# First attention of a hybrid encoder: weights turned by VectorE in 32x32 blocks and moved by DMA in place of TensorE transposes

## What is computed

```python
z = einsum('bhqd,bkhd->bhqk', qi, k) * scale
mask = kpos[None, :] < qpos[:, None]
log_1m = where(mask, log_sigmoid(-z), 0.0)
suffix = cumsum(log_1m, axis=3, reverse=True) - log_1m
w = where(mask, exp(log_sigmoid(z) + suffix), 0.0)
out = einsum('bhqk,bkhd->bqhd', w, v)
```

## Time and profile before

| | |
|---|---|
| median of three runs | 1105.87 us (1105.68 to 1105.93) |
| the profiled execution's own time | 1106.12 us |
| its span, first to last instruction | 1104.3 us |
| TensorE busy | 1096.4 us, 99% of the span |
| VectorE busy | 646.1 us, 59% |
| ScalarE busy | 472.8 us, 43% |
| GpSimd busy | 9.6 us, 1% |
| data moved by DMA | 105.11 MB, 95 GB/s on average |
| granted TensorE clock | 0.999 of full speed |

### The profile page before, as it was taken

The page is one execution under the profiler, slowest core; times in us unless marked ns, Lnnn a source line. Parts: engine busy times, 40 slices in busy tenths (PEclk is TensorE's granted clock), DMA queues, the critical chain, the costliest instruction groups (busy, mean ns, idle before and its releaser), DMA issues.

```text
span 1104.3 us, 14616 instructions
## 1 busy us (share of the span) xinstructions
PE 1096.4 (99%) x5336; PEld 900.5 (82%) x5336; DVE 646.1 (59%) x812; ACT 472.8 (43%) x705; POOL 9.6 (1%) x28
## 2 busy tenths in 40 slices
PE   9999999999999999999999999999999999999998
PEld 7788777888888888888888887888888888888886
DVE  6454456656777777763335567656777777762232
ACT  5547437444434444432223456634434444431132
POOL 2000000000000000000000000000000000000000
PEclk9999999999999999999999999999999999999999
DMA  5333131322222222233335221222233222323322
GB/s 199 134 115 96 39 96 39 112 97 92 99 97 95 95 95 95 78 84 100 91 99 159 75 77 58 77 86 90 99 101 100 95 95 95 95 77 119 102 85 77
DMA packets 33017, 105.11 MB, mean 95 GB/s; under 512 B 3905, under 2 KB 4562, under 8 KB 32978
## 3 DMA queue, kind: packets, MB, share of 16 engines
q1 hardware_dynamic: 32258, 103.58, 28.9%
q10 hardware_dynamic: 720, 0.99, 0.3%
HBM read 100.36 MB, written 2.10 MB: 93 GB/s over the span
## 4 chain that ended last, share of the span: by engine, by line
PE 96%; ACT 1%; DVE 1%; DMA 1%; issue 1%; SPq 1%; DVEq 0%; ACTq 0%
PE ps L1318 30%; PE ps L1320 30%; PE ps L1319 29%; PE ps L1517 1%; PE ps L1538 1%; PE ps L1635 1%; PE ps L1660 1%; DMA w_raw<-w_mix 1%; PE ps L1530 1%; PE ps L1645 1%; DVE ssq L954 1%; SPq L507 0%; PE ps L1589 0%; PE ps L1456 0%; PE ps L1577 0%
## 5 line engine op out<-in xcount | busy, mean ns | idle before, releaser
L1318 PE MATMUL ps<-h_hi,w_hi 128*128 128x512 f32 x888 | 349.7, 394 | 0.3 <-DVE h_lo L959 0.3
L1320 PE MATMUL ps<-h_hi,w_lo 128*128 128x512 f32 x888 | 345.9, 390 | 0.0
L1319 PE MATMUL ps<-h_lo,w_hi 128*128 128x512 f32 x888 | 345.7, 389 | 0.0
L655 ACT ACTIVATE w_hi<-w_raw 128x1024 fp32r<-128x1024 f32 (+2 forms) x136 | 135.9, 999 | 420.7 <-PE ps L1320 420.7
L941 DVE TENSOR_TENSOR w_lo<-w_raw,w_hi 128x1024 fp32r<-128x1024 f32 (+2 forms) x136 | 156.0, 1147 | 168.2 <-ACT w_hi L655 167.8
L1318 PEld LDWEIGHTS ps<-h_hi,w_hi 128*128 128x128 f32 x888 | 166.7, 188 | 36.5 <-issue 1.5
L1320 PEld LDWEIGHTS ps<-h_hi,w_lo 128*128 128x128 f32 x888 | 166.7, 188 | 35.1
L1319 PEld LDWEIGHTS ps<-h_lo,w_hi 128*128 128x128 f32 x888 | 166.8, 188 | 34.1 <-issue 0.5
L1109 DVE TENSOR_TENSOR us<-ps,rinv 128x512 f32<-128x512 f32 x88 | 60.7, 692 | 83.4 <-PE ps L1320 83.4
L662 ACT ACTIVATE w_hi<-w_raw 128x1024 fp32r<-128x1024 f32 x47 | 49.3, 1056 | 72.4 <-PE ps L1320 72.2
L947 DVE TENSOR_TENSOR w_lo<-w_raw,w_hi 128x1024 fp32r<-128x1024 f32 x47 | 57.2, 1221 | 35.1 <-ACT w_hi L662 35.0
(11 more groups left out here) (219 smaller groups left out, 1329.8 us busy)
## 6 DMA issues: line engine op xcount, KB each, us to landing
w_raw<-w_up SPq DMA_DIRECT2D x88, 512.0 KB, 3.3
w_raw<-w_mix SPq DMA_DIRECT2D x51, 512.0 KB, 3.4
w_raw<-w_down SPq DMA_DIRECT2D x22, 512.0 KB, 3.3
w_raw<-w_down SPq DMA_DIRECT2D x16, 384.0 KB, 3.1
w_raw<-w_down SPq DMA_DIRECT2D x16, 320.0 KB, 2.9
x<-xT SPq DMA_DIRECT2D x8, 256.0 KB, 6.5
out<-x SPq DMA_DIRECT2D x6, 256.0 KB, 2.0
w_raw<-w_mix SPq DMA_DIRECT2D x4, 256.0 KB, 5.4
```

What stands on the lines that cost most here:

```text
L655: s.activation(w_hi[r % SPL][:, 0:cols], w_raw[r][:, 0:cols], ACT.Copy).then_inc(w_hi_ready, 1)
L1318: mm(dst, w[0], m[0], start=first, stop=False, skip_group_check=shared)
L1319: mm(dst, w[0], m[1], start=False, stop=False, skip_group_check=shared)
L1320: return mm(dst, w[1], m[0], start=False, stop=last, skip_group_check=shared)
```

## The change

VectorE turns each head's weights in 32x32 blocks (`v.transpose`) into a new tile, `sbT`, which lies where `oc_lo` lies later. A 32x32 block is then right in itself but stands in the wrong row group, so SyncE issues 16 transfers a head (`move`), one for each pair of row groups: 32 partitions by ten blocks by 32 words, from `sbT` to `sbW`. The TensorE step "turn" and ScalarE's copy are gone. VectorE's next transpose waits for the transfers of the head before. "pv" reads the blocks in the order that they now have, with five matmuls a head.

The mask is no longer added to the scores. GpSimd sets the blocks on the diagonal of `sbG` to zero on and above it, with two selects a head, after ScalarE's second sigmoid and before VectorE's product; `sbR` holds ones on and above the diagonal, so that the scan gives one there.

Loads of the first mixer's units from the sixth on are issued by ScalarE at the step "split" in place of SyncE. SyncE's swaps and moves stand in one order, worked out from the list (`swap_at`). `EVENTS0` is new. At the start the first two units come in three pieces each, one of them issued by ScalarE, x comes first and from a layout with whole blocks, and there are 11 warm-up matmuls. The diff, cut to its core:

```diff
-EVENTS0 = ((0, "split", 2), (16, "sq", 0), (16, "sq", 1), (21, "split", 3), (24, "ssq", 0), (26, "split", 4),
...
+EVENTS0 = ((7, "split", 2), (20, "sq", 0), (25, "split", 3), (26, "sq", 1), (26, "split", 4), (28, "ssq", 0),
+           (31, "split", 5), (32, "rinv", 0), (33, "split", 6), (35, "left", 0), (37, "z", 0), (44, "split", 7),
+           (44, "z", 1), (46, "split", 8), (53, "move", 0), (53, "left", 1), (55, "split", 9), (76, "split", 10),
+           (76, "split", 11), (76, "split", 12), (89, "pv", 0), (89, "move", 1), (89, "z", 2), (89, "gt", 0),
+           (90, "gz", 0), (92, "left", 2), (93, "split", 13), (96, "gz_v", 0), (97, "split", 14), (102, "split", 15),
+           (102, "move", 2), (105, "gs", 0), (106, "z", 3), (106, "left", 3), (109, "gd", 0), (109, "move", 3),
+           (115, "split", 16), (115, "z", 4), (122, "left", 4), (122, "split", 17), (123, "gd_v", 0),
+           (125, "split", 18), (127, "left", 5), (127, "pv", 1), (127, "z", 5), (132, "split", 19), (138, "move", 4),
+           (146, "split", 20), (153, "split", 21), (157, "move", 5), (161, "gkv_v", 0), (162, "gkv", 0),
+           (162, "z", 6), (163, "left", 6), (166, "split", 22), (170, "gkv_v", 1), (171, "split", 23),
+           (172, "go_v", 0), (174, "move", 6), (174, "gkv", 1), (174, "pv", 2), (177, "go", 0), (181, "go", 1),
+           (181, "z", 7), (181, "go_v", 1), (182, "gn", 0), (183, "left", 7), (184, "gn_v", 0), (188, "split", 24),
+           (188, "gn", 1), (189, "split", 25), (196, "silu", 0), (199, "gout", 0), (199, "move", 7),
+           (200, "split", 26), (201, "pv", 3), (201, "gn_v", 1), (202, "silu", 1), (212, "gout", 1))
...
-def swap_before(j):
-
-    steps = [(name, i) for name, i, _ in SEQ0]
-    before = steps[:steps.index(("z", 2 * j - 1))] if j else []
-    running = max([i for name, i in before if name == "unit"], default=0)
-    return max(running, MIX0.index(("kb", j))) + RAW + 1
+def swap_at(j):
+
+    keys = max(n for n, step in enumerate(SEQ0) if step[:2] in [("unit", MIX0.index((w, j))) for w in ("qb", "kb")])
+    before = [n for n, step in enumerate(SEQ0) if step[:2] == ("z", 2 * j - 1)]
+    return max([keys] + before) + 1
...
-ZOFF = (0, 640, 1024, 512)
-ZW = (512, 384, 256, 128)
+OWN_PAIRS = ((128, 384), (768, 256))
+PV_PARTS = ((0, 0, 3, 0), (0, 896, 1, 3), (1, 128, 3, 0), (2, 256, 2, 0), (3, 384, 1, 0))
...
+        before_gla = ExitStack()
+        sbT = sb("sbT", [P, ZN], F32, before_gla)
+        before_gla.close()
...
-        WARM = 14
+        N_CONSTS = 18
+        WARM = 11
...
+        PIECES = (slice(0, 2 * P), slice(2 * P, 4 * P), slice(4 * P, UC))
+        BLOCK_PIECE = {0: 0, 2: 1}
 
         def load_x(engine, c):
 
-            engine.dma_start(x[:, c, :], xT[:, c * T:(c + 1) * T]).then_inc(x_loaded[c], 16)
-
-        def load_half(engine, u, half):
-
-            engine.dma_start(w_raw[u][:, W_HALVES[half]], w_mix0[u][:, W_HALVES[half]]).then_inc(
-                w_loaded[u] if half else half_loaded[u], 16)
-
-
+            engine.dma_start(x[:, c, :], xT[c]).then_inc(x_loaded[c], 16)
+
+        def load_piece(engine, u, n):
+
+            engine.dma_start(w_raw[u][:, PIECES[n]], w_mix0[u][:, PIECES[n]]).then_inc(
+                w_loaded[u] if n == 2 else piece_loaded[u][n], 16)
...
-            load_half(sp, 0, 0)
             load_x(sp, 0)
-            load_half(sp, 1, 0)
-            for c in (1, 2, 3):
+            load_piece(sp, 1, 0)
+            load_x(sp, 1)
+            load_piece(sp, 0, 1)
+            load_piece(sp, 1, 1)
+            for c in (2, 3):
                 load_x(sp, c)
-            load_half(sp, 0, 1)
+            load_piece(sp, 0, 2)
             load_x(sp, 4)
-            load_half(sp, 1, 1)
+            load_piece(sp, 1, 2)
...
+            def move(i):
+
+                sp.wait_ge(sb_turned, i + 1)
+                sp.wait_ge(sb_pv, i // 2)
+                to, turned = (t[:, :].rearrange("p (n q) -> p n q", q=P) for t in (sbWs[i % 2], sbT))
+                for a in range(TT):
+                    for b in range(TT):
+                        sp.dma_start(to[quad(b), :, quad(a)], turned[quad(a), :, quad(b)]).then_inc(sb_moved, 16)
+
+            unit(RAW, 0, w_mix0[RAW])
+            for at, (name, i, _) in enumerate(SEQ0):
                 for j in range(SH // 2):
-                    if u == swap_before(j):
+                    if at == swap_at(j):
                         swap_halves(j)
+                if name == "move":
+                    move(i)
+            for u in range(N0 + SPL + RAW - 1, U_UP0):
...
-                last = QOFF[i] + (i + 1) * P - 1
-                step(g.memset(sbR[:, last:last + 1], 1.0))
+                own = sbR[:, QOFF[i] + i * P:QOFF[i] + (i + 1) * P]
+                step(g.affine_select(out=own, in_=own, compare_op=ALU.is_gt, fill=1.0,
+                                     base=0, pattern=[[-1, P]], channel_multiplier=1))
...
+            inverse_root(0)
+            for i in range(SH):
+                pool.wait_ge(sb_gate, i + 1)
+                for at, stride in OWN_PAIRS:
+                    own = sbG[:, at:at + 2 * stride].rearrange("p (a k) -> p a k", a=2)[:, :, stride - P:stride]
+                    ins = g.affine_select(out=own, in_=own, compare_op=ALU.is_gt, fill=0.0,
+                                          base=0, pattern=[[0, 2], [-1, P]], channel_multiplier=1)
+                    ins.then_inc(sb_masked, 1)
+            for norm in range(1, 2 * LAYERS):
+                inverse_root(norm)
...
+            load_piece(act, 0, 0)
...
+            first_h_hi(0)
+            piece_hi(0, 0)
+            piece_hi(1, 0)
+            first_h_hi(1)
...
+                    u = i + RAW - 1
+                    act.wait_ge(w_lo_ready, u - (RAW - 1))
+                    act.dma_start(w_raw[u % RAW][:, :], w_mix0[u]).then_inc(w_loaded[u % RAW], 16)
                     hi_static(i)
...
-                    act.wait_ge(sb_z, i + 1)
+                    act.wait_ge(sb_z, TT * (i + 1))
+                    act.wait_ge(sb_weight, i)
                     s.activation(sbA[:, 0:ZN], zs[:, 0:ZN], ACT.Sigmoid, scale=-1.0).then_inc(sb_rest, 1)
+                    act.wait_ge(sb_turned, i)
                     s.activation(sbG[:, :], zs[:, 0:ZN], ACT.Sigmoid).then_inc(sb_gate, 1)
-                elif name == "turn":
-                    act.wait_ge(sb_turned, i + 1)
-                    act.wait_ge(sb_pv, i // 2)
-                    s.activation(sbWs[i % 2][:, :], zs[:, 0:ZN], ACT.Copy).then_inc(sb_w, 1)
...
-                    dve.wait_ge(sb_gate, i + 1)
+                    dve.wait_ge(sb_masked, 2 * (i + 1))
                     v.tensor_tensor(sbG[:, :], sbG[:, :], sbA[:, 1:ZN + 1], ALU.mult).then_inc(sb_weight, 1)
+                    dve.wait_ge(sb_weight, i + 1)
+                    dve.wait_ge(sb_moved, MOVED * i)
+                    v.transpose(sbT[:, :], sbG[:, :]).then_inc(sb_turned, 1)
...
+                        dve.wait_ge(sb_moved, MOVED * SH)
...
-                    pe.wait_ge(consts_dve, 1)
-                    pe.wait_ge(sb_w, i)
+                    pe.wait_ge(sb_gate, i)
...
-                           start=b != 0, stop=False, skip_group_check=True)
-                    for b in range(TT):
-                        diag_block = QOFF[b] + b * P
-                        ins = mm(zs[:, diag_block:diag_block + P], ident_bf[:, :], negmask[:, :],
-                                 start=False, stop=True, skip_group_check=True)
-                    ins.then_inc(sb_z, 1)
-                elif name == "turn":
-
-                    pe.wait_ge(sb_weight, i + 1)
-                    for b in range(TT):
-                        for k in range(b + 1):
-                            at, src = ZOFF[k] + (b - k) * P, QOFF[b] + k * P
-                            ins = nc.tensor.transpose(zs[:, at:at + P], sbG[:, src:src + P], ident[:, :])
-                    ins.then_inc(sb_turned, 1)
+                           start=b != 0, stop=True, skip_group_check=True).then_inc(sb_z, 1)
                 elif name == "pv":
-                    pe.wait_ge(sb_w, 2 * i + 2)
+                    pe.wait_ge(sb_moved, MOVED * (2 * i + 2))
                     pe.wait_ge(oc_lo_ready, i)
-                    for b in range(TT):
+                    for b, at, n, to in PV_PARTS:
                         for hh, w in enumerate(sbWs):
                             h = 2 * i + hh
-                            ins = mm(ps[SD * hh:SD * hh + SD, B_O, b * P:T], vb[:, b, h * SD:(h + 1) * SD],
-                                     w[:, ZOFF[b]:ZOFF[b] + ZW[b]], start=b == 0, stop=b == TT - 1)
+                            cells = w[:, at:at + (n - 1) * T + P] if n == 1 else w[:, :].rearrange(
+                                "p (a k) -> p a k", k=P)[:, at // P:at // P + (n - 1) * TT + 1:TT, :]
+                            ins = mm(ps[SD * hh:SD * hh + SD, B_O, to * P:(to + n) * P],
```

(48 more changed lines are left out.)

68 lines of the change are left out of this document (30 added, 38 removed).

## The result

The changed kernel takes 1114.74 us (median of six runs, 1113.1 to 1117.5) against 1105.76 us for the kernel before on the same chip: 1.0084 times as long, 95% interval 1.0073 to 1.0095. I had forecast 1096.1 us, range 1092.5 to 1112. The profiled execution took 1114.66 us, its span is 1112.9 us, 8.6 more than before.

A forecast was written before the change was run, and what follows sets the result against it. TensorE, 96% of the chain, was taken to bound the kernel. From the profiled 1106.12 us, 12.0 saved on TensorE and 2.25 of late transfers added gave 1096.4, or 1096.1 in terms of the median; range 1092.5 to 1112.

The forecast's parts named there:

- SyncE: the price that decides: SyncE's 16 transfers a head: one issued every 0.47 us, the last landing after 2.4 us, 9.45 us in all.
- a rival at 0.11: Moves on SyncE issue like the swaps, 0.61 us each: late by 8.6 us, 1102.4 us in all; chance 0.11.
- M: Time from a head's turned tile to its last transfer's landing: forecast 9.45 us, ends 7.35 and 11.55.
- rival 4: Slower: a move's issue grows with its 320 runs; at 0.9 us an issue, 21.6 us late, 1115.5 us; chance 0.24.
- Deadlines: Transfers late at pv 0, 1 and 3 by M less 8.6, 8.7, 8.8: 2.25 us in all; pv 2 in time.
- VectorE: Eight turns of 1.5 us, 12 us beside TensorE; head 1's wait for earlier transfers, some 5 us, inside the split's lead.
- TensorE: Removed: turns 8.7, mask matmuls 2.6, last copy's wait 0.9 us; added: 0.3 for pv's extra parts; net 12.0 us.
- GpSimd: Two selects a head, at most 1.2 us, hidden by 1.7 us of scan.
- rival 3: GpSimd's selects run behind the scan: weights 1.2 us later at pv 1 and pv 3, 1098.5 us; chance 0.08.
- ScalarE: Loses eight copies of 1.22 us, gains 25 weight-load issues at 0.4 us: 9.8 against 10 us, nothing.
- the start: Fewer warm-ups and smaller first pieces: taken as 0, bounds 1.2 us gained and 0.3 lost.
- The engines' own time does not bind: DMA engines moving a head's blocks: 320 runs per engine at 17 ns each, 5.5 us a head.

The follow-up runs named there:

- ScalarE's version: Changed kernel with eight of each head's sixteen transfers issued by ScalarE instead of SyncE: 1117.24 us, 1.011 of the kernel before.
- GpSimd's run: Changed kernel with eight of each head's sixteen transfers issued by GpSimd behind its selects, instead of SyncE: 1102.98 us, 0.9977 of the kernel before.
- swap 1 behind the moves: Changed kernel with swap 1 put behind head 1's sixteen transfers in SyncE's list: 1110.41 us, 1.0035 of the kernel before.
- waits filled: Changed kernel with 14 multiplications ahead of TensorE's wait for the transfers at pv 0, 1 and 3: 1113.56 us, 1.0064 of the kernel before.
- both ways out together: Changed kernel with GpSimd issuing half the transfers, swap 1 behind head 1's transfers and an early activation (table load): 1095.31 us, 0.9901 of the kernel before.

## Why the prediction was wrong

**The step that failed** is "SyncE: the price that decides". It took 0.47 us as the interval, from a row of loads at the start, and named the swaps' 0.61 as the upper end and as a rival at 0.11. Measured are 616 ns an issue and an interval of 0.66 to 0.72, so M is 12.0 to 13.9 us in place of 9.45 (at pv 3 the last landing adds to it, 3.92 us against 2.4), at the point (12.7) from which rival 4 decided. Neither the number of runs (rival 4's mechanism, which a tenth of the runs denies for all but 1 us) nor chance makes it: a transfer from SBUF to SBUF issues like a swap, and the swaps were the only rows of that kind. I had weighed the longer series above the row of the same kind. That rival 4's 1115.5 us lies near the measured 1114.74 is luck: it came from an interval of 0.9 us, which no run shows.

**Deadlines** held within about a us. M less 8.6, 8.7 and 8.8 gives 3.9, 3.3 and 5.1 us with the measured M; TensorE waited 4.30, 3.15 and 3.99, and pv 2 not at all. So the error of M is in the result three times.

**What was missing** is the clock. A stall was priced at its own length; 5.0 us of half clock stood behind the three. With the waits of the measured M and nothing else, the sum would have been -12.0 + 11.4 = -0.6 us: no change. The clock alone takes that to slower, and VectorE's wait, below, adds to it.

**VectorE.** The turn at 1.5 us was right. "For head 1 that is some 5 us, inside the lead" was wrong: VectorE stood 4.80 us, and the eviction of kb behind it made TensorE wait 2.2, and put swap 1, and with it move 1, later. I had looked at low halves and not at evictions.

**TensorE.** Turns and the last copy went as said. The masks gave 1.4 instead of 2.6, since part of the row of 0.33 moves to the next matmul; pv's two further pieces cost nothing where the clock is full (2.38 against 2.30 to 2.37 us).

**GpSimd.** Neither hidden nor 1.2 us late: 0.66 us a head on seven of eight heads. The first select beside a scan takes 1.86 us, from 84.22 to 86.08, while the scan runs from 83.06 to 85.89; two selects with no scan beside them take 0.77 us together. That is rival 3's mechanism at a smaller size.

```profile
83.06 2.83 DVE L1093 TENSOR_TENSOR_SCAN sbA<-sbA,sbR 128x1280 f32<-128x1280 f32 x1
```

```profile
84.22 1.86 POOL L677 TENSOR_SCALAR_AFFINE_SELECT sbG<-sbG 128x256 f32<-128x256 f32 x1 [37.49 <-ACT sbG L778]
```

```profile
45.96 0.77 POOL L677 TENSOR_SCALAR_AFFINE_SELECT sbG<-sbG 128x256 f32<-128x256 f32 x2 [4.89 <-ACT sbG L778]
```

The rule I weighed, in the Trainium skill, SBUF — State Buffer, "SBUF: two separate sides", that the two exclude each other for a whole instruction, agrees with these rows in the main: the select ends 0.19 us after the scan. One alone takes 0.40, so 0.19 is less than a whole select, which these rows leave open.

**ScalarE** and **the start** came out as said, near nothing: TensorE waits nowhere in the attention for ScalarE, and the start gave 0.5 us; about 1 us more was there to be had, and the table load took it.

**"The engines' own time does not bind"** held at 12 us a head, and at head 3 of ScalarE's version too, where sixteen moves are issued in 5.3 us and land after 2.5. Landings were long in both kinds of kernel where a weight load runs beside the moves: 3.92 us at pv 3 with one queue, 5.04 at head 3 with GpSimd's.

## What to carry to other kernels

Before work is moved to many small transfers, price one issue by a row of the same kind (SBUF to SBUF here, 0.6 us), multiply by the longest row of them, and lay that against every waiter, on every engine. A stall of TensorE costs its length and, where the clock falls after it, what it then runs at half clock: here 11.4 us of waits and 5.0 behind them. When the issue binds, share it between queues, and look at the place in the second queue: it gave 12 us with GpSimd and nothing with ScalarE, whose list came to the last head 10 us late. The Trainium skill, Perfetto Trace Analysis, "DMA Optimizations", says that balancing transfers over the engines that can issue them may help where generating descriptors binds. GpSimd's run agrees with it: 1114.74 to 1102.98 us.

## What the runs showed of the hardware

- An issue of an SBUF-to-SBUF transfer costs 616 ns with 320 runs and 591 with 32 (medians); on GpSimd 603 (mean). In the kernel after the swaps, with 64 runs, take 598 (`kbT`), and single weight loads from HBM and the last stores to HBM 333. The first move of heads 0, 3 and 7, which follows no other issue, takes 0.72, 0.64 and 0.58 us, so the price is not that of standing in a row, and it is not that of SBUF as a source, which the stores have too. Why this kind costs about twice a load stays open.
- In the kernel after the granted clock fell to 0.50 for about three us after the waits of 3.15 to 4.30 us at pv. After waits of 2.06 us (swap 1 behind the moves, pv 1) and 2.13 us (waits filled, pv 0) pv ran at full clock; after one of 1.93 us (waits filled, pv 3) the clock fell about a us into pv. After the wait of 1.1 us for swap 1 it fell five us later, with other matmuls between. So the length of the last wait alone does not order these rows.
- Where two queues issue a head's moves, an issue is no slower. The landing was long where a weight load is issued soon after the moves begin: 5.4 and 4.9 us at head 3 with SyncE and GpSimd (load at 109.78 us, moves from 108.07), 3.7 and 3.6 at head 0 with SyncE and ScalarE (load at 45.60, moves from 44.48). With no load among them it was as with one queue, 2.5 and 2.4 at head 3 with ScalarE, 2.1 and 2.1 at head 6 with GpSimd (both ways out together). Whether the load is the cause was not tried by itself.
